# Prompt attention: the SyncE queue serves one head at a time

## The reference

```
scores = einsum('bthd,bshd->bhts', q, k) * SCALE + cq - ck
p      = softmax(where(kpos <= qpos, scores, NEG_INF))
out    = einsum('bhts,bshd->bthd', p, v)
```

## Time and profile before

| | us |
|---|---|
| median of 3 runs | 4040.79 |
| the profiled execution's own time | 4037.74 |
| its span, first to last instruction | 4035.9 |
| stage `pa`, first matmul to barrier | 287.3 to 411.8 |
| stage `pb` | 424.8 to 604.4 |
| stage `pc` | 2233.5 to 2621.4 |

### The profile page before, as it was taken

One profiled execution on the slowest core, in us unless ns is written; L12 is line 12 of the kernel. 1 busy time (PEld: TensorE's weight loads), 2 busy tenths in 40 slices (PEclk: granted clock), 3 DMA queues, 4 the chain that ended last, 5 costly groups with the idle time before them and its releaser, 6 DMA issues. The chain is left out here.

```text
span 4035.9 us, 59973 instructions
## 1 busy us (share of the span) xinstructions
PE 3580.6 (89%) x23352; PEld 3142.4 (78%) x23352; DVE 1607.6 (40%) x2877; ACT 1144.6 (28%) x2204; POOL 257.0 (6%) x340
## 2 busy tenths in 40 slices
PE   8986775878899999996999788878888799999997
PEld 7865673657899999995899677756657799999997
DVE  5426553445333333325311444534443333333334
ACT  4224332443211111113221333344443211111111
POOL 2300000003100000004000000000001200000003
PEclk9997886989999999998999888889998899999999
DMA  5445435962311111104462544299984311111102
GB/s 171 122 137 117 114 80 178 380 239 94 94 42 31 52 42 31 52 21 135 143 189 90 106 89 89 56 358 359 353 303 167 105 31 52 42 31 52 42 21 99
DMA packets 408260, 494.99 MB, mean 123 GB/s; under 512 B 89120, under 2 KB 260272, under 8 KB 407536
## 3 DMA queue, kind: packets, MB, share of 16 engines
q1 hardware_dynamic: 408064, 492.33, 39.5%
HBM read 408.02 MB, written 85.16 MB: 122 GB/s over the span
## 5 line engine op out<-in xcount | busy, mean ns | idle before, releaser
L2314 PE MATMUL f_gate<-m_ht_hi,f_w_hi 128*128 128x384 f32 x1056 | 354.8, 336 | 25.7 <-DVE f_w_lo L2207 25.7
L2215 DVE TENSOR_TENSOR f_gated<-f_gated,f_up 128x384 f32<-128x384 f32 x132 | 73.1, 554 | 740.4 <-ACT f_gated L2148 740.4
L2239 DVE TENSOR_TENSOR f_y<-f_y,f_down 128x512 f32<-128x512 f32 x396 | 269.5, 686 | 229.7 <-PE f_down L2327 229.6
L2314 PE MATMUL f_gate<-m_ht_lo,f_w_hi 128*128 128x384 f32 x1056 | 354.4, 336 | 0.0
L2314 PE MATMUL f_gate<-m_ht_hi,f_w_lo 128*128 128x384 f32 x1056 | 354.4, 336 | 0.0
L2314 PE MATMUL f_up<-m_ht_hi,f_w_lo 128*128 128x384 f32 x1056 | 352.7, 334 | 0.0
L2314 PE MATMUL f_up<-m_ht_hi,f_w_hi 128*128 128x384 f32 x1056 | 352.7, 334 | 0.0
L2314 PE MATMUL f_up<-m_ht_lo,f_w_hi 128*128 128x384 f32 x1056 | 352.7, 334 | 0.0
L2327 PE MATMUL f_down<-f_wo_hi,f_act_hi 128*128 128x512 f32 x792 | 313.2, 395 | 10.7 <-DVE f_y L2239 9.4
L2327 PE MATMUL f_down<-f_wo_hi,f_act_lo 128*128 128x512 f32 x792 | 309.8, 391 | 0.0
L2327 PE MATMUL f_down<-f_wo_lo,f_act_hi 128*128 128x512 f32 x792 | 309.7, 391 | 0.0
(11 more groups left out here) (379 smaller groups left out, 7139.3 us busy)
## 6 DMA issues: line engine op xcount, KB each, us to landing
sc_kc<-in_cache_c_k SPq DMA_DIRECT2D x64, 1024.0 KB, 16.2
sc_vc<-in_cache_c_v SPq DMA_DIRECT2D x64, 1024.0 KB, 15.1
f_raw<-in_w_ffn_in SPq DMA_DIRECT2D x88, 512.0 KB, 5.0
sb_kc<-in_cache_b_k SPq DMA_DIRECT2D x32, 1024.0 KB, 14.6
sb_vc<-in_cache_b_v SPq DMA_DIRECT2D x32, 1024.0 KB, 14.4
f_raw_o<-in_w_ffn_out SPq DMA_DIRECT2D x22, 1024.0 KB
f_raw<-x SPq DMA_DIRECT2D x18, 512.0 KB, 4.1
abp_raw<-in_w_ab_in SPq DMA_DIRECT2D x32, 256.0 KB, 3.0
```

What stands on the lines that cost most here:

```text
L2215: dve.tensor_tensor(prod[:, b], silu[:, b], up[:, q, 0:gw], ALU.mult).then_inc(prod_done, 1)
L2239: dve.tensor_tensor(part, part, down[:, half, :], ALU.add).then_inc(added, 1)
L2314: last = pe.matmul(acc[:, q, 0:gw], a[:, s, k, u, :], b[:, k, token], start=(k == 0 and j == 0), stop=(k == KT - 1 and j == 2))
```

## The change

The loop over `e` is no longer closed after `load_qk`: the second `for e in range(2):` goes, and the three lines under it join the first loop. Nothing is added, and the numbers waited for stay the same.

```diff
@@ -918,7 +918,6 @@
                 for e in range(2):
                     sp.wait_ge(scores_done, units * i + TILES_P * (e + 1))
                     load_qk(i + 1, e)
-                for e in range(2):
                     sp.wait_ge(pv_done, 4 + units * i + TILES_P * (e + 1))
                     load(i + 1, e)
                     store(i, e)
```

## The result

The changed kernel takes 3867.87 us, the median of 4 runs (3866.31 to 3869.31), against 4039.84 us: ratio 0.957, 95% interval 0.956 to 0.959, 172 us less (the 4039.84 us are the three runs of above and a fourth). The forecast was 3869 us. The profiled execution took 3869.31 us by itself, span 3867.5: 168.4 us less than the span before.

What follows compares the result with a forecast made beforehand. TensorE, busy 89% of the span, was taken to stall at each trip's turn on head 0's late values, its clock falling too. 4037.7 minus 169.7 (`pc` 104.0, `pb` 32.9, `pa` 32.8) gave 3868.0, stated as 3869 us, range 3858 to 3889.

Steps and rivals of the forecast that it cites:

- Where the stall comes from: At each turn of a trip in `pa`, `pb`, `pc`, TensorE waits for head 0's late values; 113.3 us idle in all.
- The sum, 169.7 us: Stretches with a trip's turn minus as many without: `pc` 104.0, `pb` 32.9, `pa` 32.8 us saved.
- The clock's share, 57.4 us: Part of the 170.7 us in stretches with a turn that is TensorE's lowered clock, not idle time.
- Values and store cost `pa` 1 us: In `pa`, values have 0.9 us to spare; 1 us in all deducted for turns that miss by a little.
- Small pieces: Values and output move in 256-byte pieces; in `pa` values, sink and output ran at 215 GB/s, queries and keys at 221.
- rival A: `pa` bound by its transfers, values, sink and output at half rate: 12.0 us a head against 10.6; 3876 to 3891; chance 0.13.
- VectorE's wait for the stored buffer only comes earlier: Head 0's store, moved ahead of head 1's queries and keys: the queue is back in time, the wait costs nothing.
- When things are issued: After the queue's release, values leave at some 9 us in `pc`, 4.5 in `pa`; eighth output ends at 9.7 and 4.9.
- Rival D: Head 1's queries and keys starve behind head 0's store, making the kernel slower, 4072 us if outputs are a stretch later; chance 0.01.

Runs made afterwards that it cites:

- run 4: Kernel before, head 0's values behind the sixteenth score, ahead of head 1's queries and keys: 3913.49 us; with three of those loads ahead of the values: 3999.39 us.
- run 5: Kernel before, queue unchanged, TensorE's wait for the values moved from a head's first score to its first attend: 3945.93 us, ratio 0.978.
- run 6: Kernel before, stall kept, TensorE given 64 unused matmuls at each turn of a trip: 4016.33 us; with 76 to 90, filling the stalls: 3982.51 us.
- run 7: Changed kernel with each head's values in `pa` loaded twice, the second time into a buffer nothing reads: 3873.51 us, ratio 0.959.
- run 1: Kernel before with only the load of head 0's values moved up behind the eighth attend, its store left late: 3891.53 us, ratio 0.963.
- run 2: Kernel before with only the store of head 0 moved up, its values left late: 4038.72 us, ratio 0.999.
- run 3: Kernel before with head 0's values early, its store late, and four output buffers in place of two: 3869.82 us, ratio 0.958.

## Why the prediction was right

- *Where the stall comes from.* Right: the values of head 0. Runs 4 and 5 show it by dose and, in `pc` and `pb`, by name; the page's "issue" could not. In `pa` the sink behind them is late with them.
- *The sum, 169.7 us.* Right: 170.9 in the stretches (104.1, 33.0, 33.8 against 104.0, 32.9, 32.8). The method carried it: the stretch without a turn was a measurement of the stretch with one, free of the stall. That the median came within 1.1 us is luck in part: this execution is 1.3 us over its forecast of 3868.0 (1.2 us more won in the stretches, 2.5 us lost elsewhere), and the median is 1.4 us under the execution, where before it was 3.1 and then 2.1 us over.
- *The clock's share, 57.4 us.* Right in size: at least 55 us by run 6.
- *Values and store cost `pa` 1 us.* 0.4 us of waits. The values landed 5.9 us (median) after their issue, so some 10.5 us after the release, with 1.2 us to spare. The DMA share is 0.91 to 1.03, on average 0.96, where 9.6 / 10.6 = 0.91 was forecast: the engines moved 203 to 211 GB/s of busy time (199 / 0.96 and so on), not 218. The margin is a little thinner than it looked, and run 7 uses it up.
- *Small pieces.* The half rate of rival A was a supposition, and no run shows it. The slices of the earlier trace rows ran at 221 and 215 GB/s, 3% apart. At half rate a head of `pa` would have needed 12.0 us and takes 10.6, and run 7's extra bytes, 1.2 us a head at 218 GB/s, lengthened a stretch by 0.3 us. A loss of a few per cent is not excluded.
- *"VectorE's wait for the stored buffer only comes earlier".* Right for the change, but I priced the store's move at nothing. Runs 1 to 3 give it 24 us: it is the second of two waits in line, and the sum held only because the change moved both.
- *When things are issued.* Two readings were a unit off, in opposite directions. In `pc` the values left 7.3 us after the release (2181.10 to 2188.35), not 9, and the store 8.2 us, not 9.7: I had taken the ninth attend for the eighth, because a float32 tile of an attend shows as two matmuls (16 for the eight of the earlier trace rows). In `pa` the store left 6.0 us after the release (297.51 to 303.54), not 4.9: there I had taken the seventh output for the eighth, which ended at 302.63 before. The values' 4.5 us in `pa` still came out, at 4.6, and that is luck: from attend to output it is 1.5 us, not 0.4. Neither slip changed an answer, since the queue was free again 8.7 us before the next release in `pc` and 4.2 us in `pa`.
- *Rival D.* It never came near. The queue was back 8.7 us (2189.65 to 2198.34) before the next release in `pc`, 4.2 us (303.91 to 308.07) in `pa`.

## What to carry to other kernels

Write a queue of transfers in the order in which their waits come true, buffer by buffer; here a load behind a later wait was late by that wait and by the bytes that were put before it (a turn of `pc` idle for 1.1, 5.2 and 8.2 us with none, three and seven loads ahead). Where a loop has steps with and without a stall, the undisturbed step is the forecast, and the difference to it holds the clock's cost (here 57.4 of 170.7 us). When a stall goes, look for the waits that it covered, here a store that held the only free output buffer (24 us), and move them with it.

## What was not expected of the hardware

An idle stretch of TensorE far under 8 us cost the clock in runs 6 and 7. With 1.9 us idle in the turn of run 6 shown, the granted clock fell from 1.00 to 0.50, and four of six stretches of that run were hit (0.83); in run 7 one wait of 1.0 us was followed by a stretch at 0.86. At like waits some turns were hit and some not: of the two stretches of run 6 shown, 1.2 us of idle time went with a clock of 0.83 and 1.7 us with 1.00, and with the stalls filled to the end waits of 1.0 us in `pc` and 1.2 us in `pa` left it at 1.00. What decides is open.
